# A two-block transformer on one core: router fed with raw rows, joint selection for both token tiles, first pair of experts gathered ahead of the branch

## The chip, the cores and the metric

One NeuronCore of one Trainium2 chip runs the whole program, 1 launch. The metric is the device time in microseconds of that core, the median of the runs.

## The reference, cut to what matters

256 tokens of 1024 columns in fp32 pass through two blocks. The first has two layers, each a hybrid mixer (attention and retention) and an FFN; layer 0's FFN is dense, layer 1's has 8 experts, of which each token takes the best two. The second has two layers of FFN, mixer (even, then odd) and FFN.

```python
h = rms_norm(x, norm_ffn_g[l]) * (1.0 + sc2) + sh2
logits = h @ w_router                      # 1024 x 8
top_logits, top_idx = top_k(logits, 2)
top_w = softmax(top_logits)
f[token] = sum over the two of top_w * swiglu(h[token], w_gate[e], w_up[e], w_down[e])
x = x + g2 * f
```

## The kernel before

Tokens lie on the 128 partitions, in two tiles t = 0, 1. Every fp32 weight product is made of three passes of a rounded format: a weight unit of 128x1024 is split by ACT into its high part (`hi`, L319) and by DVE into the rest (`lo`, L321), and `passes` (L339) multiplies high by high, high by low and low by high. SP loads units into 12 raw buffers and waits for the `lo` that frees one; 6 split buffers stand behind them. `split_to(n)` (L331) queues splits up to unit n, on ACT and DVE at the place in program order where it is called; a split of unit u waits until PE has used unit u - 6. All engines run their queues in program order, and the order of the work is written out by hand: `slot(n)` (L1363) hangs side work behind the n-th unit of a mixer, `late` and `run_late` (L742) postpone the additions to x of tile 1.

**End of a mixer.** `out_second` (L442) multiplies the last four units, first all four for tile 0, then `between()`, then all four for tile 1. Unit i belongs to column half i // 2. `gated_add` (L905) adds a half of a tile to x: with a gate a multiplication and an addition on DVE, without one a single operation. Tile 0's additions wait for all four units of the tile, tile 1's, which are late, for the last unit.

**Norm.** The hybrid layers use `normed_modulated` (L872): sum of squares on ACT, rstd, scaling on DVE, 8 transposes by PE, then scale and shift into `hT_full` and the split into `aT`, in pairs of columns. Two splits of units stand before it. The second block uses `normed_plain` (L885): raw rows are transposed, `plain_tile` (L770) scales them, then the sum of squares, `run_late`, and `split_to(use + 4)`; PE starts with the units of tile 0, and tile 1 is transposed behind the second unit.

**Router.** `route` (L2142) runs `normed_modulated` for both tiles, then 16 router matmuls (8 columns wide, in fp32; each is two records) for both tiles into one bank, then for each tile a chain of small operations: copy, best 8, their indices, conversion, softmax of two, the weights by expert (L2155 to L2172). Five small matmuls (L2177) give each token its slot within its expert and the number of tokens of the busiest expert.

**Branch.** `moe` (L2193) lets PE, ACT and DVE wait for the busiest count and for all banks, load it into registers (L2226) and branch (L2228, L2232): above 128 tokens every expert works on all tokens (`experts_on_all_tokens`, L2256), else on up to 128 gathered slots (`experts_on_slots`, L2311), which is what this run does. There, A, B and V are the counters of ACT, PE and DVE. Before expert 0: split of the normed rows of both tiles (L2471), four one-hots (L2474), two gathers of 16 matmuls through banks 6 and 7, each followed by four scale-and-shift pieces on ACT into `x_pair` (L2399), and the split of the first expert's 128 slots (L2415). The 8 experts then take 11 steps each (4 units gate and up, 2 units down), the last six of an expert in a loop of 3 rounds of two steps (L2516).

## Time and profile before

| | us |
|---|---|
| runs, median (lowest to highest of 3) | 2460.24 (2458.99 to 2460.8) |
| the profiled execution | 2462.99 |
| its span | 2461.6 |
| PE busy in the span | 2311.1 |
| DVE busy | 1710.0 |
| ACT busy | 1418.9 |
| mean granted clock of PE, share of full speed | 0.964 |

The span runs from the first to the last instruction of the profiled execution; all positions in the text are microseconds from its start. Granted clock 1.00 is 2.4 GHz and 0.50 is 1.2 GHz. Matmuls are pipelined: the start of the next one is the better measure of their pace. "idle before, <- X" means that the engine waited for X.

### The profile page before, as it was taken

What the parts mean: (1) busy time and instruction counts of PE and PEld (TensorE: products, weight loads), DVE (VectorE), ACT (ScalarE), POOL (GpSimd) and SP (SyncE); (2) the same over time, 40 slices, a digit from 0 to 9 for tenths busy, and PEclk for the clock granted to TensorE, in tenths of its full rate; (3) what the DMA queues carried; (4) which work ended last, traced back from release to release, by engine and by line L of the source; (5) the groups of instructions that cost most, each with busy time, mean ns of one, the idle gap of its engine ahead of it and who ended that gap; (6) DMA issues with size and microseconds to landing.
All of it is one profiled execution on the core that took longest, in us unless ns stands there. A gap on an engine that the chain in (4) does not pass through costs nothing.

```text
span 2461.6 us, 34926 instructions
## 1 busy us (share of the span) xinstructions
PE 2311.1 (94%) x10627; PEld 1894.7 (77%) x10627; DVE 1710.0 (69%) x2227; ACT 1418.9 (58%) x2081; POOL 42.4 (2%) x69
## 2 busy tenths in 40 slices
PE   6998998994999999999999799989999999889998
PEld 5777887774788888888888678867788788667887
DVE  4777787773799998998999755566555555654554
ACT  4545445553777777778777554455544544565443
POOL 1000110000000000000000000000000000000000
PEclk8999999996999999999999999998999999989999
DMA  8855985842899999999999845543555465411651
GB/s 300 275 171 191 312 289 206 290 131 53 285 366 350 352 366 353 355 363 350 366 353 366 289 154 189 192 147 104 162 187 188 156 195 179 135 61 60 205 192 48
DMA packets 411195, 571.46 MB, mean 232 GB/s; under 512 B 28103, under 2 KB 324465, under 8 KB 410962
## 3 DMA queue, kind: packets, MB, share of 16 engines
q1 hardware_dynamic: 401200, 543.13, 66.2%
q0 software_dynamic: 6960, 23.79, 3.1%
q10 hardware_dynamic: 2930, 3.22, 0.4%
q8 instruction: 56, 0.92, 0.2%
q14 instruction: 49, 0.40, 0.1%
HBM read 568.98 MB, written 1.05 MB: 232 GB/s over the span
## 4 chain that ended last, share of the span: by engine, by line
PE 85%; DVE 7%; ACT 5%; issue 2%; DMA 1%; SPq 1%; ACTq 0%; DVEq 0%
PE bank L342 75%; DVE lo L321 2%; PE bank L531 1%; ACT xn L102 1%; PE bank L2352 1%; PE bank L2404 1%; ACT aT_hi L102 1%; PE bank L766 1%; ACT hi L319 1%; SPq L268 1%; PE bank L2460 1%; DVE xn L102 1%; DVE small L102 1%; ACT L102 1%; DVE x_res L102 0%
## 5 line engine op out<-in xcount | busy, mean ns | idle before, releaser
L321 DVE TENSOR_TENSOR lo<-raw,hi 128x1024 fp32r<-128x1024 f32 x997 | 1178.0, 1222 | 185.6 <-ACT hi L319 171.0
L319 ACT ACTIVATE hi<-raw 128x1024 fp32r<-128x1024 f32 x997 | 1003.8, 1054 | 103.7 <-PE bank L342 95.2
L342 PE MATMUL bank<-hi,aT_hi 128*128 128x512 f32 (+1 forms) x2016 | 816.0, 405 | 31.7 <-ACT proj L102 12.3
L342 PE MATMUL bank<-hi,aT_lo 128*128 128x512 f32 (+1 forms) x2016 | 793.0, 393 | 0.0
L342 PE MATMUL bank<-lo,aT_hi 128*128 128x512 f32 (+1 forms) x2016 | 791.9, 393 | 0.0
L342 PEld LDWEIGHTS bank<-hi,aT_hi 128*128 128x128 f32 x2016 | 384.8, 191 | 114.3 <-ACT proj L102 13.4
L342 PEld LDWEIGHTS bank<-hi,aT_lo 128*128 128x128 f32 x2016 | 384.0, 190 | 81.9
L342 PEld LDWEIGHTS bank<-lo,aT_hi 128*128 128x128 f32 x2016 | 385.7, 191 | 74.7 <-issue 1.7
L342 PE MATMUL bank<-hi,hidT_hi 128*128 128x512 f32 x792 | 311.8, 394 | 6.8 <-DVE hidT_lo L541 5.8
L342 PE MATMUL bank<-lo,hidT_hi 128*128 128x512 f32 x792 | 310.8, 392 | 0.0
L342 PE MATMUL bank<-hi,hidT_lo 128*128 128x512 f32 x792 | 310.5, 392 | 0.0
L342 PEld LDWEIGHTS bank<-hi,hidT_hi 128*128 128x128 f32 x792 | 150.1, 190 | 39.8 <-DVE hidT_lo L541 7.6
L342 PEld LDWEIGHTS bank<-hi,hidT_lo 128*128 128x128 f32 x792 | 150.2, 190 | 31.6
L342 PEld LDWEIGHTS bank<-lo,hidT_hi 128*128 128x128 f32 x792 | 150.2, 190 | 30.9
L520 DVE SCALAR_TENSOR_TENSOR hid<-silu_g,r_keep,bank 128x256 f32<-128x256 f32 x88 | 41.9, 476 | 159.8 <-ACT silu_g L510 159.8
L510 ACT ACTIVATE silu_g<-bank,r_keep 128x256 f32<-128x256 f32 x88 | 41.4, 471 | 180.5 <-PE bank L342 180.5
L539 ACT ACTIVATE hidT_hi<-bank 128x512 fp32r<-128x512 f32 x55 | 32.9, 598 | 182.3 <-PE bank L531 182.3
L541 DVE TENSOR_TENSOR hidT_lo<-bank,hidT_hi 128x512 fp32r<-128x512 f32 x55 | 38.1, 692 | 136.4 <-ACT hidT_hi L539 136.4
L2340 ACT ACTIVATE silu_g<-bank 128x256 f32<-128x256 f32 x88 | 33.9, 385 | 111.2 <-PE bank L342 111.2
L102 ACT ACTIVATE aT_hi<-bank,cols_sb 128x128 fp32r<-128x128 f32 (+1 forms) x104 | 29.3, 390 | 64.1 <-PE bank L766 58.4
L2358 ACT ACTIVATE hidT_hi<-bank 128x256 fp32r<-128x256 f32 x88 | 34.0, 386 | 50.3 <-PE bank L2352 50.3
L986 DVE SCALAR_TENSOR_TENSOR acc_sum<-ada_slot,c_cols,acc_sum 128x512 f32<-128x512 f32 x70 | 52.6, 751 | 6.8 <-DMA ada_slot<-ada_w 4.5
(289 smaller groups left out, 1634.8 us busy)
## 6 DMA issues: line engine op xcount, KB each, us to landing
raw<-moe_w_gate SPq DMA_DIRECT2D x352, 256.0 KB
raw<-moe_w_up SPq DMA_DIRECT2D x352, 256.0 KB
raw<-moe_w_down SPq DMA_DIRECT2D x176, 512.0 KB
raw<-ffn_w_gu SPq DMA_DIRECT2D x352, 256.0 KB
raw<-ffn_w_down SPq DMA_DIRECT2D x110, 512.0 KB
raw<-ada_w SPq DMA_DIRECT2D x56, 512.0 KB
raw<-w_in SPq DMA_DIRECT2D x56, 512.0 KB
ada_slot<-ada_w POOLq DMA_DIRECT2D x40, 512.0 KB, 5.9
```

Source lines behind the costliest of these rows:

```text
L102: return self.did(op(*args, **kw))
L268: sp.dma_start(dst(raw[slot]), src).then_inc(raw_full[slot], 32 // len(parts))
L319: act.activation(hi[u % SPL][:, :], raw[r % RAW][:, :], ACTF.Copy).then_inc(hi_done, 1)
L321: dve.tensor_tensor(lo[u % SPL][:, :], raw[r % RAW][:, :], hi[u % SPL][:, :].bitcast(F32), ALU.subtract).then_inc(lo_done, 1)
L342: ins = pe.matmul(bank, left[a], right[b], start=first and n == 0, stop=last and n == 2)
L510: act.activation(silu_g[:, t, :], psum[t][:, 0:STEP_F], ACTF.Silu, scale=scale(t) if scale else 1.0).then_inc(ffn["ev"].silu, 1)
L520: ins = dve.scalar_tensor_tensor(out=hid[:, t, :], in0=silu_g[:, t, :], scalar=weight(t), in1=up, op0=ALU.mult, op1=ALU.mult)
L539: act.activation(hidT[0][:, :], psum[2][:, :], ACTF.Copy).then_inc(ffn["ev"].hi, 1)
L541: dve.tensor_tensor(hidT[1][:, :], psum[2][:, :], hidT[0][:, :].bitcast(F32), ALU.subtract).then_inc(ffn["ev"].lo, 1)
L986: ins = dve.scalar_tensor_tensor(out=acc[:, :], in0=src, scalar=c, in1=acc[:, :], op0=ALU.mult, op1=ALU.add)
L2340: act.activation(silu_g[:, g % 2, :], psum[g % 2][:, 0:STEP_F], ACTF.Silu).then_inc(ev.silu, 1)
L2358: act.activation(hidT[0][:, 0:S], psum[2][:, 0:S], ACTF.Copy).then_inc(ev.hi, 1)
```

## The change

- The router's weights are loaded in layer 1's mixer (slot 2) and kept; at slot 6 `fold_router` multiplies them by the norm's modulated gain and computes the shift's share of each logit. The router then takes transposed raw rows, and rstd is applied to the logits.
- Tile 0's raw rows are transposed inside `out_second`, behind the third unit of tile 1. `rest` does the remainder: late additions, tile 1's transposes, router matmuls for each tile, split of the scaled rows straight from x.
- Selection, slots and weights are made for both tiles in one operation each; four small matmuls remain. The softmax comes behind the gather.
- One-hots, gathers of the first pair (32 matmuls into banks 6, 7, 4, 5), scale and shift on ACT and DVE in turn, and the first expert's split by column pairs stand ahead of the branch. The other branch makes its norm itself.
- In `out_second`, for all four mixers, the additions wait by column halves, and splits are queued up to `u + 7`, that is three units past the mixer's four, of which one or more stood before.

```diff
-    top_idx = sb("top_idx", [P, 8], U32)
+    top_idx = sb("top_idx", [P, NT, 8], U32)
+    router = sb("router_sb", [P, KD, NE])
+    router_g = sb("router_g", [P, KD, NE])
+    router_b = sb("router_b", [P, NE])
...
-    def out_second(left, marks, between=lambda: None, gate=None):
+    def out_second(left, marks, between=lambda: None, gate=None, inside=lambda i: None):
...
             ins = out_unit(u, i, 0, left, False, True)
-        mark0 = PE.did(ins)
+            if i == 1:
+                mark00 = PE.did(ins)
+        mark01 = PE.did(ins)
         between()
+        for half in range(2):
+            bank_mark[4 + half] = gated_add(0, half, psum[4 + half][:, :], (mark00, mark01)[half], gate)
         for i in range(4):
             out_unit(u, i, 1, left, False, True).then_inc(unit_free, 1)
+            inside(i)
         st["use"] += 4
-        for half in range(2):
-            bank_mark[4 + half] = gated_add(0, half, psum[4 + half][:, :], mark0, gate)
+        split_to(u + 7)
 
         def add_second(half):
-            bank_mark[6 + half] = gated_add(1, half, psum[6 + half][:, :], (unit_free, u + 4), gate)
+            bank_mark[6 + half] = gated_add(1, half, psum[6 + half][:, :], (unit_free, u + 2 * half + 2), gate)
...
+    def fold_router():
+        prod, rows_of_b = tiny(KD * NE), tiny(NE)
+        by_k = prod.rearrange("p (k e) -> p k e", k=KD)
+        DVE.need(router_in[0], *mod_marks)
+        a = DVE.did(dve.tensor_tensor(router_g[:, :, :], router[:, :, :], gain_cols[:, 8:16].unsqueeze(2).to_broadcast([P, KD, NE]), ALU.mult))
+        b = DVE.did(dve.tensor_tensor(by_k, router[:, :, :], mod_cols[:, 16:24].unsqueeze(2).to_broadcast([P, KD, NE]), ALU.mult))
+        b = DVE.run([b], dve.reduce_sum, rows_of_b, prod.rearrange("p (k e) -> p e k", k=KD), axis=AX.X)
+        PE.need(b, *bank_mark[7])
+        m = PE.did(pe.matmul(psum[7][:, 0:NE], ones_sq[:, :], rows_of_b, start=True, stop=True))
+        m = DVE.run([m], dve.tensor_copy, router_b[:, :], psum[7][:, 0:NE])
+        bank_mark[7] = (m,)
+        route["folded"] = [a, m]
...
                 fetch_gates(1, x_mark)
+                router_in[:] = [fetch("router_in", (), (router[:, :, :], io["router_w"][0].rearrange("(k p) e -> p k e", p=P)))]
+            if n == 6 and layer:
+                fold_router()
...
+        def inside(i):
+            if layer and i == 2:
+                route["rstd"](0)
+                route["turn"](0, 0)
+                route["turn"](0, 1)
+        out_second([a[:, 4:8, :] for a in aT], chain["T"], between, 0, inside)
...
-    def route():
-
-        rm = fetch("router_in", x_mark[0:1], (router[:, :, :], io["router_w"][0].rearrange("(k p) e -> p k e", p=P)))
...
-        return [*marks, wt, b]
+    def route_tokens():
+        r, r_mark, xT_marks, logits, parts = {}, {}, {}, {}, {}
+        top, idx = tiny(NT * 8), tiny(NT * 8)
+        top3, idx3 = (v.rearrange("p (t n) -> p t n", t=NT) for v in (top, idx))
+        def turn(t, half):
+            b = ((2, 3), (0, 1))[t][half]
+            PE.need(half_mark[t, half], *bank_mark[b])
+            for kk in range(4):
+                k = 4 * half + kk
+                ins = pe.transpose(psum[b][:, kk * P:(kk + 1) * P], x[:, t, k * P:(k + 1) * P], ident)
+            m, dst = PE.did(ins), hT_full[:, 4 * half:4 * half + 4, t * P:(t + 1) * P]
+            src = psum[b][:, :].rearrange("p (k s) -> p k s", k=4)
+            m = DVE.run([m], dve.tensor_copy, dst, src) if half else ACT.run([m], act.activation, dst, src, ACTF.Copy)
+            bank_mark[b] = xT_marks[t, half] = (m,)
+        def rstd(t):
+            r[t], r_mark[t] = rstd_tile(t)
+        def split(t):
+            h = ACT.run([r_mark[t]], act.activation, xn_split[0][:, t, :], x[:, t, :], ACTF.Identity, scale=r[t])
+            parts[t] = DVE.run([h, r_mark[t]], dve.scalar_tensor_tensor, out=xn_split[1][:, t, :], in0=x[:, t, :], scalar=r[t],
+                               in1=xn_split[0][:, t, :].bitcast(F32), op0=ALU.mult, op1=ALU.subtract)
+        def score(t):
+            PE.need(*xT_marks[t, 0], *xT_marks[t, 1], *route["folded"])
             for k in range(KD):
+                ins = pe.matmul(psum[2 + t][:, 0:NE], hT_full[:, k, t * P:(t + 1) * P], router_g[:, k, :], start=k == 0, stop=k == KD - 1)
+            logits[t] = PE.did(ins)
+        def best(t):
+            lg = tiny(NE)
+            a = DVE.run([logits[t], r_mark[t]], dve.scalar_tensor_tensor, out=lg, in0=psum[2 + t][:, 0:NE], scalar=r[t],
+                        in1=router_b[:, :], op0=ALU.mult, op1=ALU.add)
+            bank_mark[2 + t] = (a,)
+            a = DVE.run([a], dve.max, top3[:, t], lg)
+            return DVE.run([a], dve.max_index, top_idx[:, t, :], top3[:, t], lg)
+        def choose(marks):
+            eq, w = tiny(NT * 2 * NE), tiny(NT * 2 * NE)
+            eq4, w4 = (v.rearrange("p (t i e) -> p t i e", t=NT, i=2) for v in (eq, w))
+            by_tile = [v[:, 0:2 * NE].rearrange("p (e t) -> p t e", t=NT) for v in (picked, slot_of, expert_w)]
+            a = DVE.run(marks, dve.tensor_copy, idx3, top_idx[:, :, :])
+            a = DVE.run([a], dve.tensor_tensor, eq4, table("iota8").unsqueeze(1).unsqueeze(1).to_broadcast([P, NT, 2, NE]),
+                        idx3[:, :, 0:2].unsqueeze(3).to_broadcast([P, NT, 2, NE]), ALU.is_equal)
+            a = DVE.run([a], dve.tensor_tensor, by_tile[0], eq4[:, :, 0, :], eq4[:, :, 1, :], ALU.add)
+            PE.need(a, *bank_mark[3])
+            pe.matmul(psum[3][:, 16:32], table("before"), by_tile[0], start=True, stop=False)
+            m = PE.did(pe.matmul(psum[3][:, 24:32], ones_sq[:, :], by_tile[0][:, 0], start=False, stop=True))
+            for t in range(NT):
+                ins = pe.matmul(psum[3][:, 32:40], ones_sq[:, :], by_tile[0][:, t], start=t == 0, stop=t == NT - 1)
+            m = PE.did(ins)
+            s = DVE.run([m], dve.scalar_tensor_tensor, out=by_tile[1], in0=psum[3][:, 16:32].rearrange("p (t e) -> p t e", t=NT),
+                        scalar=1.0, in1=by_tile[0], op0=ALU.add, op1=ALU.mult)
+            route["slots"] = s
+            n = DVE.run([m], dve.reduce_max, busiest[:, :], psum[3][:, 32:40], axis=AX.X)
+            bank_mark[3] = (n,)
+            return eq4, w4, by_tile[2], n
+        def weights(eq4, w4, out):
+            e, r2 = tiny(NT), tiny(2 * NT)
+            by_i = r2.rearrange("p (t i) -> p t i", t=NT)
+            a = DVE.run([], dve.tensor_tensor, e, top3[:, :, 1], top3[:, :, 0], ALU.subtract)
+            a = ACT.run([a], act.activation, e, e, ACTF.Exp)
+            b = DVE.run([a], dve.tensor_scalar, by_i[:, :, 1], e, 1.0, None, ALU.add)
+            b = DVE.run([b], dve.reciprocal, by_i[:, :, 0], by_i[:, :, 1])
+            b = DVE.run([b], dve.tensor_tensor, by_i[:, :, 1], by_i[:, :, 0], e, ALU.mult)
+            b = DVE.run([b], dve.tensor_tensor, w4, eq4, by_i.unsqueeze(3).to_broadcast([P, NT, 2, NE]), ALU.mult)
+            return DVE.run([b], dve.tensor_tensor, out, w4[:, :, 0, :], w4[:, :, 1, :], ALU.add)
+        def first_pair():
+            for z in range(2):
+                for t in range(NT):
+                    hot = one_hot(DVE, z, t, 2 * z + t)
+            split_to(st["use"] + 4)
+            mark = {}
+            for i, b in enumerate((6, 7, 4, 5)):
+                PE.need(hot, parts[0], parts[1], *bank_mark[b])
+                for kk in range(2):
+                    k = 2 * i + kk
+                    for n, (t, part) in enumerate(((0, 0), (0, 1), (1, 0), (1, 1))):
+                        ins = pe.matmul(psum[b][:, kk * S:(kk + 1) * S], xn_split[part][:, t, k * P:(k + 1) * P],
+                                        onehot[:, t, :, :].rearrange("p z s -> p (z s)"), start=n == 0, stop=n == 3)
+                mark[i] = PE.did(ins)
+            out, hi_mark, lo_mark = {}, {}, {}
+            def shift(i):
+                b = (6, 7, 4, 5)[i]
+                for k in (2 * i, 2 * i + 1):
+                    op = full_dve if i % 2 else full_act
+                    out[i] = op([mark[i]], x_pair[:, k, :], psum[b][:, (k % 2) * S:(k % 2 + 1) * S], gain_cols[:, 8 + k:9 + k],
+                                mod_cols[:, 16 + k:17 + k])
+                bank_mark[b] = (out[i],)
+            def part(i, which):
+                src, dst = x_pair[:, 2 * i:2 * i + 2, 0:P], [a[:, 2 * i:2 * i + 2, 0:P] for a in aT]
+                if which == 0:
+                    hi_mark[i] = ACT.run([out[i]], act.activation, dst[0], src, ACTF.Copy)
+                else:
+                    lo_mark[i] = DVE.run([hi_mark[i]], dve.tensor_tensor, dst[1], src, dst[0].bitcast(F32), ALU.subtract)
+            shift(0)
+            shift(1)
+            part(0, 0)
+            part(0, 1)
+            shift(2)
+            part(1, 0)
+            part(1, 1)
+            shift(3)
+            part(2, 0)
+            part(2, 1)
+            part(3, 0)
+            part(3, 1)
+            route.update(hot=hot, pair=[out[i] for i in range(4)], first=[lo_mark[i] for i in range(4)])
+        def rest():
+            run_late(1)
+            turn(1, 0)
+            score(0)
+            split(0)
+            run_late()
+            turn(1, 1)
+            best(0)
+            rstd(1)
+            score(1)
+            split_hi = split
+            b = best(1)
+            eq4, w4, out, n = choose([b])
+            split_hi(1)
+            first_pair()
+            busy = DVE.run([n], dve.tensor_copy, busiest_i[:, :], busiest[:, :])
+            route["weights"] = weights(eq4, w4, out)
+            route["r"] = r
+            return busy
+        route.update(turn=turn, rstd=rstd, rest=rest)
+    def one_hot(V, z, t, c):
+        return V.run([route["slots"]], dve.tensor_scalar, onehot[:, t, z, :], table("iota"), slot_of[:, c:c + 1], -1.0, ALU.subtract,
+                     ALU.is_equal)
+    def moe():
...
-        marks = [*marks, *(m for b in range(8) for m in bank_mark[b])]
+        busy = route["rest"]()
+        PE.need(*(m for b in range(4) for m in bank_mark[b]))
         for e in (PE, ACT, DVE):
-            e.need(*marks)
+            e.need(busy)
...
+        VA.need(*route["pair"], *route["first"], route["weights"])
+        AA.need(*route["pair"])
+        PA.need(*route["pair"], *route["first"])
+        for t in range(NT):
...
-                    c = 2 * (2 * p + z) + t
-                    m = V.run([], dve.tensor_scalar, onehot[:, t, z, :], table("iota"), slot_of[:, c:c + 1], None, ALU.is_equal)
+                    m = one_hot(V, z, t, 2 * (2 * p + z) + t)
...
-        h = A.run([], act.activation, xn_split[0][:, :, :], xn[:, :, :], ACTF.Copy)
-        m = V.run([h], dve.tensor_tensor, xn_split[1][:, :, :], xn[:, :, :], xn_split[0][:, :, :].bitcast(F32), ALU.subtract)
-        B.need(m)
-        one_hots(0)
-        gather(0, 0)
-        gather(0, 1)
-        split_expert(0)
+        hot[0], gathered[0], bank_67[0] = (route["hot"],), route["pair"], route["pair"]
...
-                B.need(*aT_ready[0])
-                gate_up(0, 0, 0, 0)
-                gate_up(2, 0, 0, 0)
+                gate_up(0, 0, 0, 0, route["first"])
+                gate_up(2, 0, 0, 0, route["first"])
...
+                if e == 0:
+                    B.need(*route["pair"], route["weights"])
...
+    route_tokens()
     hybrid_mixer(1)
-    moe(route())
+    moe()
```

## Rows read from the trace of the kernel before

**Rows 1.** The page, part 1: busy time, share of the span, instructions of each engine.

```profile
PE 2311.1 (94%) x10627; PEld 1894.7 (77%) x10627; DVE 1710.0 (69%) x2227; ACT 1418.9 (58%) x2081; POOL 42.4 (2%) x69
```

**Rows 2.** Busy time by stretch (us, times): engines, then granted clock, transfers' share, GB/s.

```profile
564.93:621.06 56.13, 20.74 (x92) 19.23 (x91) 21.93 (x63) 21.47 (x47) 4.62 (x9) 0.52 0.19 41
700.00:800.00 100.00, 100.00 (x468) 82.85 (x467) 91.15 (x100) 79.72 (x104) 0.00 (x0) 1.00 1.06 356
```

**Rows 3.** The chain that ended last, 544 to 650 us: start, us, what.

```profile
582.57 6.98 PE bank L2151 x32
...
595.19 2.32 PE bank L2179 x10
...
601.97 1.92 ACT xn_hi L102
...
603.91 2.29 DVE xn_lo L102
606.20 0.80 DVE onehot L102 x4
...
607.13 3.77 PE bank L2404 x16
...
616.73 1.94 ACT x_pair L102 x4
...
621.06 10.53 PE bank L342 x36
```

**Rows 4.** Instructions in order of time, DVE, 562 to 577 us.

```profile
562.26 0.69 DVE L102 TENSOR_TENSOR x_res<-x_res,xn 128x512 f32<-128x512 f32 x1
564.61 2.36 DVE L321 TENSOR_TENSOR lo<-raw,hi 128x1024 fp32r<-128x1024 f32 x2 [1.65 <-ACT hi L319]
...
571.07 0.68 DVE L102 TENSOR_TENSOR xn<-bank,gates 128x512 f32<-128x512 f32 x1
...
573.45 0.69 DVE L102 TENSOR_TENSOR x_res<-x_res,xn 128x512 f32<-128x512 f32 x1
...
576.03 0.16 DVE L102 RECIPROCAL small<-small 128x1 f32<-128x1 f32 x1 [1.22 <-ACT small L102]
```

**Rows 5.** Groups with shapes kept apart, whole span, bank to SBUF: busy us, mean ns.

```profile
L102 ACT ACTIVATE proj<-bank 128x512 f32<-128x512 f32 x28 | 16.3, 596 | 19.6 <-PE bank L342 19.6
...
L102 DVE COPY qkT<-bank 128x512 f32<-128x512 f32 x8 | 5.1, 679 | 0.0
```

**Rows 6.** The same view, 582 to 600 us.

```profile
L102 DVE MAX8 small<-small 128x8 f32<-128x8 f32 x2 | 0.3, 171 | 0.1
```

**Rows 7.** Source lines 2226 and 2232, PE's queue at the branch: ns min/median/max, start.

```profile
L2226 PEldq TENSOR_LOAD <-busiest_i x1: 487/487/487, 598.3 to 598.3; - x1
...
L2232 PEldq COMPARE_BRANCH  x1: 3928/3928/3928, 598.8 to 598.8; - x1
```

**Rows 8.** Instructions in order of time, PE (last row ACT), 1611 to 1618 and 1728 to 1738 us.

```profile
1611.54 1.03 PE L766 MATMUL bank<-tables_sb,x_res 128*128 128x128 f32 x8
...
1617.08 0.48 PE L342 MATMUL bank<-hi,aT_hi 128*128 128x512 f32 x1
...
1728.15 1.04 PE L766 MATMUL bank<-tables_sb,x_res 128*128 128x128 f32 x8
...
1734.04 0.50 PE L342 MATMUL bank<-hi,aT_hi 128*128 128x512 f32 x1 [2.49 <-DVE lo L321]
...
1737.69 0.73 PE L342 MATMUL bank<-hi,aT_hi 128*128 128x512 f32 x1
...
1728.57 2.17 ACT L102 ACTIVATE aT_hi<-bank,cols_sb 128x128 fp32r<-128x128 f32 x8 [12.71 <-PE bank L766]
```

**Rows 9.** Instructions in order of time, DVE, layer 1's mixer, 442 us.

```profile
442.01 1.22 DVE L321 TENSOR_TENSOR lo<-raw,hi 128x1024 fp32r<-128x1024 f32 x1
```

**Rows 10.** Instructions in order of time, PE, a gather inside the expert stage.

```profile
738.92 0.28 PE L2404 MATMUL bank<-onehot,xn_lo 128*128 128x256 f32 x1
739.04 0.28 PE L2404 MATMUL bank<-onehot,xn_hi 128*128 128x256 f32 x1
```

More of the change, by code:

```diff
@@ L194, in program @@
     slot_w = sb("slot_w", [P, 2])
-    router = over("router_sb", [P, KD, NE], at_qkT)
     hT_full = over("hT_full", [P, KD, S], at_probs)
@@ L1415, in between @@
             close_accs(bank=1)
-        out_second([a[:, 4:8, :] for a in aT], chain["T"], between, 0)
+        def inside(i):
[4 more added lines that the diff above has]
+        out_second([a[:, 4:8, :] for a in aT], chain["T"], between, 0, inside)
         if layer:
@@ L2275, in step @@
             pe_down(u + UNITS_GU, g - 1, lap)
+        VA.need(*route["pair"], *route["first"], route["weights"])
+        AA.need(*route["pair"])
+        PA.need(*route["pair"], *route["first"])
+        for t in range(NT):
+            m = VA.run([], dve.tensor_scalar, xn[:, t, :], x[:, t, :], route["r"][t], None, ALU.mult)
+            PA.need(m)
+            for k in range(KD):
+                ins = pe.transpose(psum[k // 4][:, (k % 4) * P:(k % 4 + 1) * P], xn[:, t, k * P:(k + 1) * P], ident)
+            m = PA.did(ins)
+            for k in range(KD):
+                a = VA.run([m], dve.tensor_scalar, hT_full[:, k, t * P:(t + 1) * P], psum[k // 4][:, (k % 4) * P:(k % 4 + 1) * P],
+                           gain_cols[:, 8 + k:9 + k], mod_cols[:, 16 + k:17 + k], ALU.mult, ALU.add)
+            src, dst = hT_full[:, :, t * P:(t + 1) * P], [v[:, :, t * P:(t + 1) * P] for v in aT]
+            h = AA.run([a], act.activation, dst[0], src, ACTF.Copy)
+            PA.need(VA.run([h], dve.tensor_tensor, dst[1], src, dst[0].bitcast(F32), ALU.subtract))
         zero_y()
@@ L2326, in gate_up @@
             for j in (j0, j0 + 1):
+                if marks:
+                    B.need(marks[j])
                 pe.wait_ge(lo_done, split_end(u + j) + 12 * lap)
```

52 lines of the change are left out of this document (5 added, 47 removed).

## The prediction

> **What bounds the kernel now.** I read the page first: PE is busy 94% of the span [rows 1], so time can only be won where PE stands still or runs slowly. The busy time by stretch shows both. In the expert stage PE is busy 100 of 100 us at the full granted clock, with the transfers near their limit beside it [rows 2]; nothing of this change touches a step of that loop. Between the last matmul of the second mixer (564.93) and the first of expert 0 (621.06) lie 56.1 us in which PE is busy 20.7 us at a mean granted clock of 0.52, nearly all of it at 1.2 GHz, DVE 21.9 and ACT 21.5 us [rows 2]: no engine is full, so a serial chain sets this stretch. The chain of waits names it [rows 3]: router matmuls, two tiles' selections one after the other, the five small matmuls that number the slots, then the branch, and only behind the branch the split of the normed rows, the one-hots, two gathers of four banks' worth through two banks, and the high and low part of the first expert's input. The same kind of gap, smaller, follows the even and the odd mixer (below).
>
> **The stretch before expert 0, step by step.** I replay the new order on the clock of the old trace. Where a queue is in program order, an instruction starts when the one before it and its releaser have ended.
>
> Until 562.95 nothing differs: the gates are ready only after PE's matmul behind tile 0, so the earlier mark for the first column half gives nothing here; tile 0's rows end where they did [rows 4]. PE now transposes these raw rows between the third and the fourth unit of tile 1: 8 transposes, about 1.0 us of PE, which ends the mixer at 565.9 instead of 564.9. One copy on ACT (0.60) and one on DVE (0.68) [rows 5] end near 565.1. The two weight splits on DVE, before at 564.61 [rows 4], move to 565.65 and end at 568.0. The modulation and split of eight pieces per tile, between the old splits and the late additions, are gone from this place.
>
> The first late half (a multiplication and an addition, 0.69 each) then ends at 569.4; it stood at 571.07 [rows 4]. Four transposes at 1.2 GHz take 1.0 us, to 570.4. The router matmuls of tile 0 are half of the 6.98 us [rows 3], so 3.5 us, to 573.9; beside them ACT copies and writes the high part of tile 0 (to 572.05), DVE the low part (to 573.35; 1.22 to 1.25 for 1024 columns [rows 9]). Here the order costs something: the second late half stands behind that low part in DVE's queue, and ends at 574.75, later than its old 574.14 [rows 4]. Then four transposes to 575.8, a DVE copy to 576.5, and tile 1's router matmuls to 580.05. Its rstd (about 1.9 us from the last addition to the reciprocal before [rows 4]) is ready by 577.3, off the path.
>
> Selection: a DVE operation on 8 columns is worth 0.17 to 0.20 [rows 6]; tile 1's best (3 operations and a value load) and the joint choice (3) give 1.3 us, to 581.35. The softmax's eight steps and the trips to ACT have left the path. Four matmuls instead of five: 2.32 x 4/5 = 1.9 [rows 3], to 583.25; slots and busiest 0.35, to 583.6. The low part of tile 1 comes behind them in DVE's queue, 1.25 us, to 584.85; four one-hots 0.85 (0.80 before [rows 3]), to 585.7. The old path came out of its five small matmuls only at 597.5 [rows 3].
>
> Gathers: 32 matmuls into four banks without a pause. Sixteen took 3.77 us with their tail [rows 3], so 0.21 each: 6.9 us, to 592.6. ACT and DVE empty three of the four banks beside them. Behind the last bank stand two DVE pieces (ACT's four took 1.94 [rows 3], so I take 0.4 each), a high part, a low part (0.42 each) and the conversion of the busiest count: to 594.9. The router-weighted part (softmax, with an Exp table load on ACT) is queued behind that conversion. PE does not wait for it; ACT and DVE reach the branch 1 to 2 us after PE, and the fifth and sixth split they owe PE would come near 603, when PE needs them at about 606.5 (24 matmuls after its start). That cover would be gone if the weights took 3 us more.
>
> Branch: PE loads the count in 0.49 us and then stands 3.93 us at the branch itself [rows 7]; nothing in the change shortens this. PE's first expert matmul comes at 594.9 + 4.5 = 599.4 instead of 621.06 [rows 3]: **-21.6 us**. In this the removed split of both tiles behind the branch is 4.2 us (1.92 + 2.29) and the stop for ACT between the two gathers 1.94 [rows 3]; the rest is the tiles' modulation, the second selection, and a router that no longer waits for both tiles. The refill of the weight buffers starts again when the fifth split is done, about 4 us after PE's start rather than 1.3; the twelve loaded units cover 17 us, so I cost this at nothing.
>
> **The other mixers.** Splitting to use + 7 ahead changes nothing where the split already stands at use + 5 and the norm asked for the same units anyway (layers 0 and 1). After the even mixer it does. PE starts the transposes at 1728.15, works one unit, waits 2.49 us for a split that DVE finishes behind all of tile 0 and the late additions, has by then fallen to 1.2 GHz, and reaches its third unit at 1737.69: 9.54 us [rows 8]. The plain pattern, with splits already there, stands at the end of the block before: 1611.54 to 1617.08, 5.54 us [rows 8]. ACT was idle for 12.7 us before 1728.57 [rows 8], so two more splits (two took DVE 2.36 [rows 4]) fit beside tile 1's matmuls. That is 4.0 us, and the odd mixer shows the same pair of waits once more (2 such places): **-8.0 us**. The halves' earlier marks lie beside PE's matmuls and are worth nothing.
>
> **What is added elsewhere.** In layer 1's mixer: a 32 KB load issued from ACT's queue after the gates' loads (0.4 us of ACT beside a full PE), and the folding at the seventh slot. PE waits there for three small DVE operations (0.7 us) behind the split of 442.01 (1.22 [rows 9]); PE would reach the place at about 443.6, DVE be ready at 443.9, and the matmul itself takes 0.2: **+0.5 us**, bounds 0 (DVE finds room) and 2 (behind one more accumulation and split).
>
> **Sum.** -21.6 - 8.0 + 0.5 = -29.1 us. Span 2461.6 gives 2432.5; the profiled execution took 2462.99, 1.4 around its span, which gives 2433.9; the median shown is 2460.24, 2.75 under that execution, so **2431.1**.
>
> Bounds of what the trace does not show. The clock: PE's router matmuls, 6.98 us without a pause, stayed at 1.2 GHz, and so did the gathers of 3.8 us. If the 6.9 us of gathers rise half-way, a matmul costs 0.12 (as at 739.04 [rows 10]) instead of 0.21, 1.4 us less; and if PE stays up from the mixer's end through tile 0's router matmuls, 2 to 3 us less again. Together -5: 2426. I take the low clock, by the nearest rows. On the other side every hand-over may be 0.1 us longer over some 25 of them, and the DVE pieces of the pair may take 0.6: +4.
>
> The Trainium skill (TensorE: Matmul & The Clock Gate, "Why this matters for your kernels") says that continuous work brings the fast clock back. The old router matmuls speak against it for small matmuls; for the long gather this page would take the sum to about 2430.
>
> **Rivals.**
> 1. The chain before expert 0 shortens by less. Late additions and DVE's order may hold tile 1 longer: if the split of tile 0, the unit splits and both late halves queue up, each costs a DVE slot of 1.2 us, and PE's transposes and router matmuls follow late. Some 7 us given back: 2438. For it: DVE is in order and carries three roles here. Against: its busy total in the stretch was 21.9 of 56. 0.15.
> 2. The mixers' ends give nothing, because another late item (fourth split, late additions before tile 1's transposes) holds the third unit as long: 2431 + 8 = 2439. Against: the plain pattern has these items too and makes 5.54. 0.07.
> 3. The rearrangement does not do what it says: gathering ahead of the branch merely moves 14 us from one side to the other, since the count is converted behind it. Then only selection, norm and split are won, and the pause of 3.93 us may grow because the block that is jumped over has grown: gain some 12, at 2448. 0.03.
> 4. Slower. The branch row shows that a jump to code not at hand costs PE 3.93 us [rows 7]. The expert stage has 8 loops of 3 rounds, 24 rounds, and today no row of it shows such a wait (100 of 100 us busy [rows 2]). The change moves all of this code. If the jumps back began to cost as much, 9 of them (34 us) would make it slower, and all 24 would give 2431 + 94 = 2525. Against: the loop bodies themselves are unchanged. 0.03. The Trainium skill (Runtime: NRT & Kernel Launch, "Instruction fetch mechanics") says a taken branch outside what is loaded stops for a fetch; the row of the branch agrees, the loops show none.
>
> **How the numbers follow.** Forecast 0.72, the rivals 0.15, 0.07, 0.03 and 0.03. The range goes from 2425 (the clock's bound) to 2440 (rivals 1 and 2), and leaves out rivals 3 and 4 and the tails. 0.2% (5 us) is about what a measurement of this kernel can tell from no change: faster 0.96, same 0.01, slower 0.03.
>
> **What would show it.** Right: first expert matmul near 599 if the mixer starts when it did (0.5 later with the folding); router matmuls of the two tiles about 6 us apart, starting near 570.5 and 576.5; 32 gathers without a wait between; still one branch of 3.9 us on PE; third unit 5.5 us after the first transpose at the even and the odd mixer, the granted clock staying at 1.00 there. Wrong: a wait of PE above 1 us in the middle of a gather or at units five and six of expert 0, a wait for a split after either mixer, or any pause in the expert loops.

## The result and the profile after

| | before | after |
|---|---|---|
| runs beside each other, median (lowest to highest of 4 each), us | 2459.61 (2457.37 to 2460.8) | 2442.45 (2438.9 to 2445.38) |
| profiled execution, its span | 2462.99, 2461.6 | 2445.38, 2444.1 |
| mean granted clock of PE | 0.964 | 0.967 |

The ratio is 0.9931 (95% interval 0.9913 to 0.9948). Run again later, the same kernel took 2439.79 us (2437.09 to 2440.16; label r_after). So the change gains 17 to 20 us where 29.1 were forecast, and 2442.45 lies above the range.

To find the place I cut both traces at four marks: the last addition to x of layer 0's FFN; tile 0's last addition in layer 1's mixer [rows 4]; the first expert matmul; the experts' first addition to x. The table gives the lengths between them, with those of the experiments told below.

| kernel | to layer 0's end | layer 1's mixer | to expert 0 | experts | the rest | span |
|---|---|---|---|---|---|---|
| before | 422.59 | 139.67 | 58.80 | 784.59 | 1055.95 | 2461.6 |
| after | 426.86 | 151.17 | 36.63 | 786.63 | 1042.81 | 2444.1 |
| r_after | 422.29 | 150.61 | 36.63 | 787.94 | 1041.33 | 2438.8 |
| b2_fold_alone | 422.89 | 151.08 | 57.32 | 786.48 | 1050.13 | 2467.9 |
| b1_splits_ahead | 427.09 | 140.77 | 56.98 | 787.93 | 1041.13 | 2453.9 |
| a1_early_load | 423.72 | 145.76 | 36.64 | 786.00 | 1041.88 | 2434.0 |
| a3_router_first | 425.64 | 146.06 | 36.64 | 784.68 | 1043.08 | 2436.1 |
| a2_late_fold | 423.84 | 148.00 | 36.78 | 786.73 | 1041.75 | 2437.1 |
| d1_sum_later | 423.42 | 139.88 | 37.11 | 786.43 | 1041.66 | 2428.5 |
| d2_given_load | 423.93 | 138.52 | 36.60 | 784.54 | 1043.21 | 2426.8 |
| a4_no_splits_ahead | 422.59 | 150.00 | 34.22 | 786.21 | 1049.48 | 2442.5 |
| e2_after_splits_at_ends | 424.18 | 150.60 | 33.02 | 786.15 | 1041.95 | 2435.9 |
| d3_order | 425.26 | 141.21 | 33.79 | 786.50 | 1043.44 | 2430.2 |
| d4_all | 423.16 | 139.89 | 27.69 | 788.99 | 1041.57 | 2421.3 |
| d5_no_splits | 425.11 | 141.09 | 26.47 | 786.53 | 1050.20 | 2429.4 |
| e1_all_splits_at_ends | 422.96 | 139.90 | 26.29 | 787.63 | 1042.02 | 2418.8 |

The first two rows say it: the stretch to expert 0 is 22.2 us shorter and the rest 13.1, as good as forecast or better; but layer 1's mixer is 11.5 us **longer**, and 4.3 and 2.0 more stand in parts where nothing of the sort was forecast. One kernel run twice differs by 4.6 us to layer 0's end (after and r_after), and two kernels with the same code in the rest by 5.8 (before and b2_fold_alone): a single part of a single profile carries that much chance of the granted clock.

One row shows where such chance comes from. In the even mixer PE stops for the same thing in every kernel; first the kernel before, then the kernel after:

```profile
1640.25 0.77 PE L342 MATMUL bank<-hi,aT_hi 128*128 128x512 f32 x1 [2.96 <-ACT proj L102]
```

```profile
1635.70 0.47 PE L344 MATMUL bank<-hi,aT_hi 128*128 128x512 f32 x1 [2.96 <-ACT proj L102]
```

Behind this stop of 2.9 to 3.0 us the first pass ran at 1.2 GHz (0.77 us) in the kernel before and in d3_order, and at 2.4 GHz (0.47) in the other fourteen. From the first of the transposes of [rows 8], at 1611.54, to 1728.15 the kernel before takes 116.6 us; the kernel after takes 112.7 (1606.99 to 1719.73), and b2_fold_alone, whose code there is that of the kernel before, 112.4 (1623.38 to 1735.76). So some 4 of the 13.1 us in the rest are not what the change was to give.

The chain of waits of the kernel after in layer 1's mixer (start, us, what):

```profile
439.88 0.36 ACTq L703
...
440.26 0.49 ACTq L703
...
440.78 13.77 DMA router_sb<-router_w
...
454.57 0.23 DVE router_g L1303
454.80 0.15 DVE small L1304
...
454.96 0.28 DVE small L102
...
455.29 0.59 PE bank L1307 x2
455.88 7.66 PE bank L344 x24
```

A 32 KB load stands on the path for 13.8 us. In the kernel before the same load, issued after the mixer with little else in flight, landed in 2.2 us. The engines beside it, instructions in order of time, first PE and then DVE:

```profile
447.52 0.39 PE L344 MATMUL bank<-hi,aT_lo 128*128 128x512 f32 x1
455.29 0.59 PE L1307 MATMUL bank<-small,ones_sq 128*128 128x8 f32 x2 [7.37 <-DVE small L102]
455.73 0.77 PE L344 MATMUL bank<-hi,aT_hi 128*128 128x512 f32 x1
456.31 0.63 PE L344 MATMUL bank<-lo,aT_hi 128*128 128x512 f32 x1
456.73 0.63 PE L344 MATMUL bank<-hi,aT_lo 128*128 128x512 f32 x1
...
461.10 0.39 PE L344 MATMUL bank<-hi,aT_lo 128*128 128x512 f32 x1
```

```profile
448.87 1.22 DVE L323 TENSOR_TENSOR lo<-raw,hi 128x1024 fp32r<-128x1024 f32 x1
454.57 0.23 DVE L1303 TENSOR_TENSOR router_g<-router_sb,gain_cols 128x64 f32<-128x64 f32 x1 [4.49 <-DMA router_sb<-router_w]
```

PE waits 7.4 us for the rows that its summing matmul needs, and behind the wait it runs at 1.2 GHz: a pass follows the last in 0.43 us instead of 0.23 until about 460, and the 24 passes of the next two units take 7.66 us instead of 24 x 0.227 = 5.4.

Where the change was to gain, the chain of waits of the kernel after, 578 to 616 us:

```profile
583.76 0.61 DVE xn L102
584.40 0.70 DVE x_res L102
585.14 0.67 PE bank L2185 x4
...
587.50 1.28 DVE xn_lo L102
588.79 0.61 DVE xn L102
589.42 0.70 DVE x_res L102
590.17 1.13 PE bank L2185 x4
...
592.16 3.57 PE bank L2202 x16
...
599.32 1.19 DVE xn_lo L102
600.51 0.80 DVE onehot L102 x4
601.35 5.50 PE bank L2262 x24
...
612.58 2.08 issue
614.66 0.77 PE bank L344
```

This answers to [rows 3]: the second tile's router matmuls, then one selection, the split, the one-hots, the gathers, the pair and the branch, in the forecast's order. The branch itself, as its source line shows it (ns least, median, most, then start):

```profile
L2362 PEldq COMPARE_BRANCH  x1: 3368/3368/3368, 611.1 to 611.1; - x1
```

The even mixer's end, PE in order of time, against [rows 8]:

```profile
1719.73 1.03 PE L772 MATMUL bank<-tables_sb,x_res 128*128 128x128 f32 x8
1721.47 0.50 PE L344 MATMUL bank<-hi,aT_hi 128*128 128x512 f32 x1 [0.70 <-DVE aT_lo L102]
...
1724.42 1.09 PE L772 MATMUL bank<-tables_sb,x_res 128*128 128x128 f32 x8
1725.27 0.48 PE L344 MATMUL bank<-hi,aT_hi 128*128 128x512 f32 x1
```

The wait of 2.49 us is gone, and the third unit follows the first transpose after 5.54 us instead of 9.54, as the plain pattern did in [rows 8]. At the odd mixer it is 5.54 us instead of 9.51. The expert loops show no pauses: over 700 to 800 us PE is busy 100.00 us at full clock, as in [rows 2].

### The profile page after: what moved, and what is told of

The parts are those of the page before. It is cut to its first block, busy times and chain, and to the rows that moved or that the text cites. A ratio compares the mean times of both kernels' runs of the same rounds, so it can differ in the third digit from the quotient of the medians.

```text
span 2444.1 us, 34902 instructions
## 1 busy us (share of the span) xinstructions
PE 2310.9 (95%) x10627; PEld 1894.0 (77%) x10627; DVE 1706.2 (70%) x2214; ACT 1412.8 (58%) x2063; POOL 42.2 (2%) x69
## 4 chain that ended last, share of the span: by engine, by line
PE 85%; DVE 7%; ACT 5%; issue 2%; DMA 1%; SPq 1%; ACTq 0%; DVEq 0%
PE bank L344 75%; DVE lo L323 2%; PE bank L537 1%; PE bank L2499 1%; ACT xn L102 1%; ACT hi L321 1%; PE bank L2606 1%; SPq L270 1%; DVE xn L102 1%; PE bank L772 1%; DVE x_res L102 1%; ACT L102 1%; DVE small L102 1%; DMA router_sb<-router_w 1%; ACT aT_hi L102 1%
## 5 line engine op out<-in xcount | busy, mean ns | idle before, releaser
L300 DVE SCALAR_TENSOR_TENSOR acc_sum<-raw,c_cols,acc_sum 128x512 f32<-128x512 f32 x70 | 52.4, 748 | 1.4
```

What stands on the lines that cost most here:

```text
L300: ins = dve.scalar_tensor_tensor(out=acc[:, :], in0=src, scalar=c, in1=acc[:, :], op0=ALU.mult, op1=ALU.add)
```

## The experiments

Times are medians with their range. Every ratio is to runs of the kernel before taken beside them; their median was 2460.93 us for the labels with a, 2461.59 for b1, d1, d2 and d4, 2460.0 for b2, d3, d5 and r_after, and 2460.05 for e1 and e2.

**Is it the folding?** This kernel puts the load and the folding alone into the kernel before.

```diff
             if n == 2 and layer:
                 fetch_gates(1, x_mark)
+                router2_in[:] = [fetch("router2_in", (), (router2[:, :, :], io["router_w"][0].rearrange("(k p) e -> p k e", p=P)))]
+            if n == 6 and layer:
+                fold_router()
```

> The kernel before with nothing of the change but the router's load behind the two gate loads and the folding at slot 6 of layer 1's mixer; its results are not used, and the router is loaded and used again as before. Theory (the load's landing and TensorE's stop for the folding cost 10 to 11 us, and that is the whole of what the forecast missed): the mixer grows from 139.7 to 150 to 152 us and the time to some 2471 us (2468 to 2474). Rival (the stage is longer in the kernel after for another reason, the output additions by halves or the chance of the granted clock): 2460 to 2464 us.

Measured: 2469.65 us (2467.78 to 2473.49), ratio 1.0036 (1.0023 to 1.0049), so 9 to 10 us slower, as expected; the mixer 151.08, PE's wait at the folding 7.12 us. The whole excess of the mixer comes with these two pieces and without anything else of the change.

**What of it is the landing?** Two kernels load earlier: at the program's start, or ahead of the two gate loads on ACT's queue. A third leaves the load and folds five slots later.

```diff
+    router_early = fetch("router_in", (), (router[:, :, :], io["router_w"][0].rearrange("(k p) e -> p k e", p=P)))
     small_in = sem("small_in")
...
-    router_in, route = [], {}
+    router_in, route = [router_early], {}
```

> The kernel after, with the load of the router's weights issued at the program's start instead of in layer 1's mixer. Theory (landing): PE stood at the folding because the 32 KB load took 13.8 us to land among the full transfers; then DVE's wait of 4.5 us for it is gone, the folding costs PE under 1 us, the clock stays up behind it, and the time falls by some 10 us, to 2432 (2429 to 2436). Rival (backlog): DVE or the folding's own chain held PE, and the rest of layer 1's loss is chance of the granted clock; then 2441 to 2443, and PE still waits several us at the folding.

Measured: 2436.46 us (2433.44 to 2437.53), ratio 0.990 (0.9886 to 0.9915). The mixer comes down by 5.4 us, not to where it was: neither the expectation (a stop under 1 us, 2432 us) nor its rival came out. PE and DVE of this kernel around the folding:

```profile
444.38 0.39 PE L344 MATMUL bank<-hi,aT_lo 128*128 128x512 f32 x1
447.57 0.60 PE L1308 MATMUL bank<-small,ones_sq 128*128 128x8 f32 x2 [2.81 <-DVE small L102]
448.02 0.77 PE L344 MATMUL bank<-hi,aT_hi 128*128 128x512 f32 x1
448.59 0.63 PE L344 MATMUL bank<-lo,aT_hi 128*128 128x512 f32 x1
```

```profile
444.27 1.54 DVE L300 SCALAR_TENSOR_TENSOR acc_sum<-raw,c_cols,acc_sum 128x512 f32<-128x512 f32 x2
445.72 1.22 DVE L323 TENSOR_TENSOR lo<-raw,hi 128x1024 fp32r<-128x1024 f32 x1
446.86 0.22 DVE L1304 TENSOR_TENSOR router_g<-router_sb,gain_cols 128x64 f32<-128x64 f32 x1
...
447.25 0.27 DVE L102 TENSOR_REDUCE small<-small 128x8 f32<-128x64 f32 x1
```

With the data long there, DVE still comes to the folding 2.1 us after PE has: two accumulations (L300, of the conditioning's sums) and a split stand ahead of it. Behind PE's stop of 2.8 us twelve passes run at 1.2 GHz here too.

> The kernel after, with the router's load issued on ACT's queue ahead of the two gate loads (1 MB) instead of behind them. If the load landed late because it stood behind the gates on the same queue, it lands in a few us (2 to 5) and the time is 2432 to 2435. If it landed late because the transfers of all queues were full, it still takes 8 us or more and the time stays within 4 us of 2442.

Measured: 2437.39 us (2433.97 to 2437.72), ratio 0.990 (0.9886 to 0.9915). Ahead of the gates the load lands in 6.5 us instead of 13.8, PE waits 2.79 us, the mixer takes 146.06: as good as the early load. The two gate loads of 512 KB each ahead of it on the queue made up 7.3 us of the landing; 6.5 is still more than the 2 to 5 us expected, and the time is 2 us above the expected range.

> The kernel after, with the folding five slots later (slot 11) and the load where it is. Theory (landing): the five units take about 16 us, longer than the 13.8 us of the landing, so PE no longer waits and the time is that of the early load, 2432 (2429 to 2436). Rival (the load itself disturbs): the load takes the place of weight transfers and later splits come late, so part of the 10 us stays whatever the slot: 2437 to 2441. Rival (backlog): no change, 2442.

Measured: 2438.82 us (2437.22 to 2443.48), ratio 0.9915 (0.99 to 0.9929). The load lands after 13.3 us, long before slot 11, and PE waits 3.46 us all the same, so 2432 us is missed again; the time is that of the rival in which the load itself disturbs, which the kernel d2_given_load below tests.

**What of it is PE's stop?** The folding is cut in two: DVE's part stays, the matmul and the copy go to a later slot.

```diff
-        PE.need(b, *bank_mark[7])
+        route["rows"] = [a, b, rows_of_b]
+
+    def fold_sum():
+
+        a, b, rows_of_b = route["rows"]
+        PE.need(b, *bank_mark[7])
...
             if n == 6 and layer:
                 fold_router()
+            if n == 12 and layer:
+                fold_sum()
```

> The kernel after with the router's load at the program's start and the folding cut in two: VectorE's part stays at slot 6, the matrix unit's summing matmul and the copy behind it go to slot 12, six units of weights (some 33 us) later. Theory (the cost of the folding is that TensorE, in order, stops for VectorE's chain: 2.81 us in the run with the early load, and then runs at 1.2 GHz for some 12 passes): the stop goes and the clock does not fall; layer 1's mixer (late addition of tile 1 to tile 0's x) comes down from 145.8 us to 140 to 141 and the time to some 2431 us (2428 to 2433). Rival (the folding's own work on VectorE delays the splits behind it, whatever TensorE does): the mixer stays at 144 to 146 us, the time at 2436 us.

Measured: 2431.48 us (2428.19 to 2435.23), ratio 0.9883 (0.9867 to 0.9899). The mixer is back at 139.88. PE in order of time at the matmul of this kernel:

```profile
462.86 0.39 PE L344 MATMUL bank<-lo,aT_hi 128*128 128x512 f32 x1
463.08 0.39 PE L344 MATMUL bank<-hi,aT_lo 128*128 128x512 f32 x1
463.31 0.28 PE L1313 MATMUL bank<-small,ones_sq 128*128 128x8 f32 x2
```

No wait, and 0.2 us to the next instruction, at full clock.

> The kernel after with the router's load left behind the two gate loads (landing some 14 us after its issue), but VectorE's part of the folding at slot 10 and the matmul at slot 12, both long after the landing. Theory (the late landing costs only through the engines that stop for it): the same as with the early load, layer 1's mixer 140 to 141 us, the time 2431 us (2428 to 2433). Rival (the load takes DMA share from the weight units it lands between): 2 to 3 us more than the run with the early load, mixer 142 to 144 us.

Here the load stays where the change puts it, DVE folds at slot 10, PE sums at slot 12. Measured: 2430.42 us (2428.0 to 2434.28), ratio 0.988 (0.9865 to 0.9896), mixer 138.52. The late landing costs nothing once no engine stops for it; the rival (a share of the transfers) falls.

**The mixers' ends.** One line alone in the kernel before:

```diff
             bank_mark[4 + half] = gated_add(0, half, psum[4 + half][:, :], mark0, gate)
+        split_to(u + 7)
```

> The kernel before with one line of the change alone, the split of the next three weight units issued ahead of the last additions of each output pass. Theory (the third unit at the even and the odd mixer's end waited for its lo part behind the additions): the stretch from the first transposes to the third unit falls from 9.5 to 5.5 us at both ends, and the time by 8 us to some 2452 us (2450 to 2455). Rival (what the earlier split gives is taken back by the clock, which falls during the transposes, or by the additions): 2459 to 2461 us.

Measured: 2453.26 us (2445.89 to 2455.7), ratio 0.9962 (0.9947 to 0.9977). The distances are 5.47 us (1729.64 to 1735.11) and 5.46 (2257.70 to 2263.16): confirmed. The same line left out of the kernel after:

> The kernel after without the splits queued ahead at a mixer's end. Forecast of record: 4.0 us for the even and 4.0 for the odd mixer, so 2450 (2448 to 2453), with the third unit again 9.5 us behind the first transpose there. Rival (hidden anyway): within 2 us of 2442.

Measured: 2445.57 us (2440.59 to 2446.71), ratio 0.9936 (0.9922 to 0.995): 3 to 6 us slower than the kernel after, not 8. The waits are back, 2.47 us at both ends, but two things differ. At the odd mixer the clock does not fall behind the wait and the distance is 8.17 us instead of 9.5; at the even mixer it is 9.18. And the table shows 34.22 instead of 36.63 us to expert 0. DVE in order of time says why, first the kernel after, then the one below that keeps the line in the second block only:

```profile
580.26 0.69 DVE L102 COPY hT_full<-bank 128x512 f32<-128x512 f32 x1 [0.26 <-PE bank L2185]
581.40 2.36 DVE L323 TENSOR_TENSOR lo<-raw,hi 128x1024 fp32r<-128x1024 f32 x2 [0.45 <-ACT hi L321]
583.68 0.68 DVE L102 TENSOR_TENSOR xn<-bank,gates 128x512 f32<-128x512 f32 x1
```

```profile
577.02 0.69 DVE L102 COPY hT_full<-bank 128x512 f32<-128x512 f32 x1 [0.27 <-PE bank L2186]
577.63 0.68 DVE L102 TENSOR_TENSOR xn<-bank,gates 128x512 f32<-128x512 f32 x1
```

In layer 1 the line itself queues two weight splits ahead of tile 1's late half, which the chain to expert 0 waits for. The three pieces add up: 9.18 - 5.54 and 8.17 - 5.54 lost at the ends, 2.4 won before expert 0, together 3.9 us slower.

```diff
-        split_to(u + 7)
+        if gate is None:
+            split_to(u + 7)
```

> The kernel after, with the splits ahead of the output additions kept in the second block (the even and the odd mixer) and left out in the two layers of the first. In the run without them anywhere the stretch from tile 0's x to the first expert matmul was 34.2 instead of 36.6 us: two splits of weights no longer stood ahead of tile 1's late half in VectorE's queue. Theory: this line gives 8 us at the mixers' ends and costs 2.4 us before expert 0; the stretch comes to 34.2 us, the part behind the experts stays at 1041 to 1043 us, the time is 2.4 us below the kernel after's 2439.8 to 2442.5, some 2438.5 (2435 to 2441). Rival (the 2.4 us were given back at expert 0's first units, whose splits come later): the stretch 34.2, the experts' part 2 us longer, 2441 us.

Measured: 2437.17 us (2435.64 to 2438.46), ratio 0.9899 (0.9881 to 0.9917); to expert 0 33.02 us, the experts' part no longer for it, the rest 1041.95. The stretch runs the same code as in a4_no_splits_ahead and is 1.2 us shorter, half of it because TensorE's branch took 3.36 us here and 3.98 there.

**A faster order before expert 0**, all on top of the mended folding and the early load. The order alone:

```diff
             score(0)
-            split(0)
             run_late()
+            split(0)
...
             score(1)
-            split_hi = split
+            split(1)
             b = best(1)
             eq4, w4, out, n = choose([b])
-            split_hi(1)
             first_pair()
```

> The kernel with all the moves less one: the busiest count is converted behind the first pair again, so that TensorE's branch lies behind the pair's last split. The order alone (late half 2 ahead of tile 0's split, tile 1's split ahead of its selection) should then give 3 to 4 us against the kernel with only the folding mended, the stretch to the first expert matmul 32 to 33 us, the time 2427.5 us (2425 to 2430). Rival (the branch is what mattered): 2430 to 2431 us, the stretch 35 us.

Measured: 2434.09 us (2431.51 to 2436.32), ratio 0.9891 (0.9875 to 0.9906). In the trace the stretch is 3.3 us shorter than without the order (33.79 against 37.11), as expected; the time does not show it and is 2.6 us longer. Its profile is 1.8 us longer to layer 0's end, 1.3 in the mixer and 1.8 in the rest than that of the kernel with only the folding mended, and the order touches none of these; it is the kernel with the low clock behind the even mixer's stop shown above. The two ranges overlap, and what the order alone is worth in time stays open. With the branch moved too:

```diff
+            busy = DVE.run([n], dve.tensor_copy, busiest_i[:, :], busiest[:, :])
             first_pair()
-            busy = DVE.run([n], dve.tensor_copy, busiest_i[:, :], busiest[:, :])
```

> The folding cut in two and loaded early, and in the stretch before expert 0 three moves: the late half 2 ahead of the split of tile 0, the split of tile 1 ahead of tile 1's selection, and the conversion of the busiest count ahead of the first pair, so that the engines' loads of it and TensorE's branch (3.4 us) lie beside the last copies and splits of the pair. Theory (TensorE waited 1.9 us for turn(1,1) behind the split, the gathers waited for the split of tile 1, and the branch stands behind the pair's last split): 3 us from the order and 3 us from the branch, the stretch from the last half of tile 0's x to the first expert matmul 30 us instead of 35.9, the time 2425 us (2422 to 2428). Rival (the first matmul waits for the pair's last split and TensorE's branch was hidden beside it as it is): only the 3 us of the order, 2428 us.

Measured: 2424.19 us (2422.59 to 2428.09), ratio 0.9857 (0.9844 to 0.987); 27.69 us to expert 0 where 30 were expected. PE in order of time, this kernel:

```profile
589.43 0.28 PE L2269 MATMUL bank<-onehot,xn_lo 128*128 128x256 f32 x1
590.74 0.47 PE L344 MATMUL bank<-hi,aT_hi 128*128 128x512 f32 x1 [1.03 <-DVE aT_lo L102]
...
594.11 0.50 PE L344 MATMUL bank<-hi,aT_hi 128*128 128x512 f32 x1 [1.08 <-issue]
...
599.42 0.50 PE L344 MATMUL bank<-hi,aT_hi 128*128 128x512 f32 x1 [1.62 <-DVE lo L323]
```

PE's queue loads the count at 586.5 (its source line), while the gathers queued before it still run to 589.7, and is past its branch before the last gather is copied. It starts on the first column pair, after a stop of 1.03 us instead of 6.74, and its first passes run at 2.4 GHz; in the kernel after they ran at 1.2. The waits behind it are the next bound: the splits of expert 0's first units are late now. The experts' part is 2.6 us longer, as much as the two waits shown (1.08 and 1.62), though that column moves by more between kernels that share its code.

> The kernel with all the moves, without the splits ahead of the output additions. If the mixers' ends give 4 us each whatever else is changed: 8 us more than with them, 2432 us (2430 to 2435). Rival (most of it comes back elsewhere, as the 3 us of the first such run let one suspect): 2427 us.

Measured: 2429.21 us (2427.53 to 2431.68), ratio 0.9867 (0.9851 to 0.9884). The rest grows by 8.6 us, the stretch shrinks by 1.2, and by the medians 5 us are lost, between the two expectations. The stretch shrinks so little because the branch took 5.65 us here and 3.50 in d4_all. Both together, the splits ahead in the second block alone:

> The kernel with all the moves, the splits ahead kept in the second block alone. Without them anywhere this stretch was 26.5 instead of 27.7 us (1.2 less, since the late half stands elsewhere already). Theory: 1.2 us less than with them in all four mixers, 2423 us (2420 to 2426), the part behind the experts 1041 to 1043 us. Rival (expert 0's first units then wait longer for their splits): 2425 us, with more than the 2.7 us of waits behind the first expert matmul.

Measured: **2419.38 us** (2416.54 to 2420.1), ratio 0.9825 (0.9807 to 0.9843), the fastest of all and below the 2420 to 2426 expected; 26.29 us to expert 0. The profile is 1.4 us shorter there and 1.4 in the experts' part than d4_all, which is less than the 4.8 us between the medians; the rest of that is not explained. Behind this row, by 612 us, no wait of PE is shown, but its passes run at 1.2 GHz until 595:

```profile
589.15 0.77 PE L344 MATMUL bank<-hi,aT_hi 128*128 128x512 f32 x1 [3.00 <-DVE small L102]
```

PE stood these 3.0 us for its branch, which by its source line took 5.44 us and ended 0.2 us before that matmul; its first 2.7 us lay beside the gathers:

```profile
L2369 PEldq COMPARE_BRANCH  x1: 5443/5443/5443, 583.5 to 583.5; - x1
```

## Why the prediction missed

**The stretch before expert 0: right.** From tile 0's last addition to the first expert matmul the forecast has 599.4 - 562.26 = 37.1 us, the trace 36.6, in both profiles of the kernel. The second late half stood behind tile 0's low part as the step said (588.71, behind 587.50). Moved by the 15.8 us by which tile 0's rows end later, the replay meets the trace step by step: router matmuls of tile 1 at 592.3 (traced 592.16), gathers at 601.5 (601.35), the count's load by PE at 610.7 (610.6). The gathers took 6.6 us (601.35 to 607.92) instead of 6.9, because the granted clock rose 5.5 us into them. From their end to the count's load the forecast's terms add up to 1.8 us and it wrote 2.3; the trace has 2.7. The branch was 3.37 us instead of 3.93.

**The mixers' ends: right in place and size.** 4.0 us each against the wait and the low clock; the line alone gave the forecast's 8 (9, interval 6 to 13, from its ratio). Of the 4.0 at the odd mixer 1.3 hang on the low clock, and that is chance: the kernel before had it there (9.51 us), the three other kernels without the line had not (8.17 to 8.19). "Splitting to use + 7 ahead changes nothing where the split already stands" was true against the kernel before, whose norm asked for the same splits at 564.61 [rows 4], and my replay carried their 2.36 us. But it hid a cost: the change had removed that norm, and without the new line the splits would have been gone from this place too. Keeping them there costs 2.4 us, and 3.6 by the trace with them in the second block only.

**What is added elsewhere: wrong, and this is the miss.** "PE would reach the place at about 443.6, DVE be ready at 443.9 [...] **+0.5 us**, bounds 0 (DVE finds room) and 2 (behind one more accumulation and split)." This is the step that failed: the cost is 10 us, 9.6 in the time with the folding alone. Three things make it up:
- DVE's queue: PE arrives 2.8 us too early even when the load is there. Counted from layer 0's end, PE came to the place as forecast (443.6 on the old clock), but DVE was ready at 446.4 and not at 443.9: I had put the folding behind the split of 442.01 [rows 9], and it stood behind the next accumulations and split of that queue. My upper bound of 2 us named just this case and was 0.8 short. In the kernel before:

```profile
443.14 1.53 DVE L298 SCALAR_TENSOR_TENSOR acc_sum<-raw,c_cols,acc_sum 128x512 f32<-128x512 f32 x2
444.60 1.22 DVE L321 TENSOR_TENSOR lo<-raw,hi 128x1024 fp32r<-128x1024 f32 x1
```

- The landing: another 7.37 - 2.81 = 4.6 us, since the load was queued behind 1 MB on its queue. I priced its issue (0.4 us) and not its arrival, although DVE's first step waits for it.
- The clock: behind the stop some ten passes at 1.2 GHz, 2.2 us.

Together 9.6, and 10.0 with the matmul itself at the low clock. The traces have the same: from layer 0's end to the mixer's next wait, for `qkT`, it is 102.5 us in the kernel before, 112.7 in the kernel after and with the folding alone, and 102.7 with the folding cut in two. The mixer's excess of 11.4 us with the folding alone holds 1.2 more, behind that wait: 38.4 us instead of 37.2. That part took 38.4 in d3_order too, where PE does not stop for the folding, and 35.8 in d2_given_load, so it is chance. With -21.6 and -8.0 the cost of 10.0 makes -19.6 us, against the measured -17.2 and -20.2.

**The rivals.** Rival 1 (the chain shortens less) fell, as did 2, 3 and 4: the chain shortened as forecast, no wait took the place of the one at the mixers' ends, the gathers did not merely move, and the loops do not pause: from 630 to 1200 us PE is busy 570 of 570 us. Rival 4 counts nine jumps as 34 us; at 3.93 each they are 35. The one branch did change where code was moved or left out: 5.65 and 5.44 us in d5_no_splits and e1_all_splits_at_ends, 3.50 in d4_all; why is not shown. The loss came from a place that no rival named, and the bounds of the small term kept it out of the range. The Trainium skill (TensorE: Matmul & The Clock Gate, "Why this matters for your kernels") says that continuous work brings the fast clock back: the gathers now agree with it, their spacing going from 0.21 to 0.12 us at 606.9; the old router matmuls, which I had put against it, ran their 7 us at the low clock without a rise.

## What to carry to other kernels

A matmul of 0.2 us put into a full TensorE stream costs as much as the latest of what it needs: before placing it, add up the queue of the engine that feeds it and the bytes ahead of its load on the same DMA queue, and let the consumer come several units later than the producer. Such a stop can be paid twice: behind each stop of 2.8 to 7.5 us at the folding came passes at 1.2 GHz, while behind one of 3.0 us elsewhere they came in some kernels and not in others, so this part is to be priced as a chance. And work that is queued "ahead" for one place of a kernel (here a weight split) should be asked for its cost in the other places that call the same function.

## What the runs showed of the hardware that was not expected

- A 32 KB load on ACT's queue landed 13.8 us after its issue behind two loads of 512 KB, 6.5 us ahead of them, and 2.2 us with little in flight. Issued at the program's start (a1_early_load) it took 13.9.
- Stops of TensorE of 2.8 and 7.4 us at the folding both brought ten to twelve passes at 1.2 GHz. At the odd mixer's end a stop of 2.5 us did so in the kernel before and did not in three other kernels (9.51 us to the third unit against 8.17, 8.18 and 8.19). Behind a stop of 3.0 us in the even mixer the first pass ran at 1.2 GHz in two kernels and at 2.4 in fourteen.
- TensorE's branch took 3.93 us in the kernel before, 3.37 in the kernel after, 3.85 with the folding cut in two, 5.44 in the fastest kernel and 5.65 in d5_no_splits. TensorE's queue goes through it while matmuls issued before it still run.
